# A second, turned copy of layer 0's rows, a begin without a meeting, and earlier first turns for the dilated stage

## The reference, cut to what matters

```python
def rms_norm(x, g):
    xf = x.astype(jnp.float32)
    y = xf * lax.rsqrt(jnp.mean(xf * xf, axis=-1, keepdims=True) + EPS) * g.astype(jnp.float32)
    return y.astype(x.dtype)

def conv_layer(x, conv_state, mem_kv, norm_g, w_in, conv_w, mem_q_g, w_out):
    b, t, _ = x.shape
    z = rms_norm(x, norm_g) @ w_in
    ...
```

```python
    s = jnp.einsum('brnqhe,brnkhe->brnhqk', qb, kk, preferred_element_type=jnp.float32)
    s = jnp.where(valid[None, None, :, None], s, NEG)
    m = jnp.max(s, axis=-1, keepdims=True)
    p = jnp.exp(s - m)
    l = jnp.sum(p, axis=-1, keepdims=True)
    o = jnp.einsum('brnhqk,brnkhe->brnqhe', p / l, vv.astype(jnp.float32)).astype(q.dtype)
```

## Time and profile before

| | us |
|---|---|
| median of 3 runs | 2821.64 (2819.12 to 2824.57) |
| the profiled execution | 2820.37 |
| its span in the trace | 2818.2 |
| TensorE busy | 2759.3 (98%) |
| VectorE busy | 1758.5 (62%) |
| ScalarE busy | 1113.7 (40%) |
| GpSimd busy | 364.9 (13%) |

### The profile page before, as it was taken

The page is one execution under the profiler, slowest core; times in us unless marked ns, Lnnn a source line. Parts: engine busy times, 40 slices in busy tenths (PEclk is TensorE's granted clock), DMA queues, the critical chain, the costliest instruction groups (busy, mean ns, idle before and its releaser), DMA issues.

```text
span 2818.2 us, 38685 instructions
## 1 busy us (share of the span) xinstructions
PE 2759.3 (98%) x13662; PEld 2278.4 (81%) x13662; DVE 1758.5 (62%) x3819; ACT 1113.7 (40%) x3357; POOL 364.9 (13%) x574
## 2 busy tenths in 40 slices
PE   7999999999999999999999999999999989989999
PEld 6787888888787888888787888788888779988887
DVE  5486666768678633325575767776765656557664
ACT  5433131222326224215434453532323348756532
POOL 0001010100101000000001132313324022210000
PEclk9999999999999999999999999999999999999999
DMA  4276555555676634324266676868777788647642
GB/s 169 86 239 199 190 186 175 183 181 176 199 244 205 202 106 145 99 99 150 94 250 229 224 245 226 286 219 286 262 267 246 253 283 286 215 151 244 200 142 95
DMA packets 282873, 559.16 MB, mean 198 GB/s; under 512 B 31168, under 2 KB 81920, under 8 KB 282680
## 3 DMA queue, kind: packets, MB, share of 16 engines
q1 hardware_dynamic: 248440, 453.89, 49.5%
q0 software_dynamic: 34240, 102.80, 10.0%
HBM read 423.85 MB, written 132.72 MB: 197 GB/s over the span
## 4 chain that ended last, share of the span: by engine, by line
PE 93%; DVE 3%; DMA 2%; ACT 1%; issue 1%; SPq 0%; DVEq 0%; ACTq 0%
PE ps L130 26%; PE ps L132 25%; PE ps L131 25%; PE ps L3560 2%; PE ps L3532 2%; PE ps L3081 2%; PE ps L3065 1%; PE ps L3569 1%; PE ps L3119 1%; PE ps L237 1%; PE ps L2122 1%; PE ps L2390 1%; PE ps L3548 1%; PE ps L3543 1%; DMA tok_b_dram<-shared_o 1%; PE ps L1149 1%
## 5 line engine op out<-in xcount | busy, mean ns | idle before, releaser
L130 PE MATMUL ps<-b_wp,b_sring 128*128 128x512 f32 x640 | 250.3, 391 | 4.4 <-DMA b_sring<-sums_dram 3.7
L131 PE MATMUL ps<-b_wp,b_sring 128*128 128x512 f32 x640 | 249.8, 390 | 0.0
L132 PE MATMUL ps<-b_wp,b_sring 128*128 128x512 f32 x640 | 249.7, 390 | 0.0
L130 PE MATMUL ps<-a_sring,a_wp 128*128 128x512 f32 x512 | 199.5, 390 | 2.6 <-DMA a_sring<-sums_a_dram 2.6
L132 PE MATMUL ps<-a_sring,a_wp 128*128 128x512 f32 x512 | 199.3, 389 | 0.0
L131 PE MATMUL ps<-a_sring,a_wp 128*128 128x512 f32 x512 | 199.2, 389 | 0.0
L132 PE MATMUL ps<-b_wp,b_xtlo 128*128 128x512 f32 x480 | 186.8, 389 | 0.0
L131 PE MATMUL ps<-b_wp,b_xthi 128*128 128x512 f32 x480 | 186.8, 389 | 0.0
L130 PE MATMUL ps<-b_wp,b_xthi 128*128 128x512 f32 x480 | 186.8, 389 | 0.0
L960 DVE TENSOR_TENSOR shared_o<-ps,b_spare 128x512 f32<-128x512 f32 x160 | 109.7, 685 | 100.5 <-PE ps L132 83.1
L802 ACT ACTIVATE ps<-shared_o 128x128 f32<-128x128 f32 (+1 forms) x408 | 108.0, 265 | 154.7 <-DVE shared_o L960 146.9
(11 more groups left out here) (461 smaller groups left out, 6823.5 us busy)
## 6 DMA issues: line engine op xcount, KB each, us to landing
b_sring<-sums_dram SPq DMA_DIRECT2D x160, 512.0 KB, 5.1
a_sring<-sums_a_dram SPq DMA_DIRECT2D x128, 512.0 KB, 5.0
b_raws<-w_b_dram SPq DMA_DIRECT2D x176, 256.0 KB, 4.3
a_raws<-w_a_dram SPq DMA_DIRECT2D x140, 256.0 KB, 4.4
kv_dram<-shared_o POOLq DMA_DIRECT2D x96, 256.0 KB, 4.2
tok_b_dram<-shared_o POOLq DMA_DIRECT2D x96, 256.0 KB, 4.5
front<-tok_b_dram SPq DMA_DIRECT2D x96, 256.0 KB, 3.7
front<-grp_dram SPq DMA_DIRECT2D x48, 260.0 KB, 4.3
```

The source lines that it names most:

```text
L130: pe.matmul(acc, a_hi, b_hi, start=first, stop=False)
L131: pe.matmul(acc, a_hi, b_lo, start=False, stop=False)
L132: return pe.matmul(acc, a_lo, b_hi, start=False, stop=last)
```

## The change

**Layer 0.** The rows come from the host in a second layout too: `x_turned` holds each tile of 128 rows turned, 1024 inputs as 8 x 128 partitions by 128 rows, and `xs_turned` the samples. A new class `TurnedPrep` takes the place of `Prep` in `mix_stage`. It still loads the rows as they are and squares them for the factors, but nothing of them is turned: VectorE puts the factors on a diagonal (`space`), TensorE multiplies that by a matrix of ones, which spreads the factors over all partitions (`spread_rows`, one matmul of 128 columns, 8 transposes before), VectorE scales the turned rows by them (`scale`, in two halves), ScalarE and VectorE make high and low part from it (`high`, `low`, in two halves). Rows have a ring of two tiles, turned rows one of three.

**Begin.** `Setup` registers the work of `setup_stage` in the common block; the engines wait for its semaphores and no longer meet. TensorE first makes 48 transposes of `ident`.

**Shared and dilated stage.** A new class `Opening` holds the buffers and steps that both stages use. Turning tile 0, the memory keys and tile 1 stand ahead of the fourth-last, third-last and second-last product of the shared stage, with their copies on ScalarE and VectorE; buffers are moved so that these rows are free by then. The masks are built eight products before the end. In the last phase of each pair the sample product and its output come one product earlier. SyncE loads tile 0, the memory keys, tiles 1 to 3, then values. It waits for the stored outputs ahead of the value of tile 4. ScalarE loads the table of exponentials ahead of the loop.

```diff
+class TurnedPrep:
...
+    TILES = NT + 1
+    ROWS, TURNED, RING = 2, 3, 4
+    HALF = KD // 2
...
+    def load_x(self, sp, t):
+        n, slot = self.rows(t), t % self.ROWS
+        if t >= self.ROWS:
+            sp.wait_ge(self.squared, t - self.ROWS + 1)
...
+    def loads(self, sp, gain_row, gain_src, gain_in):
+        self.load_x(sp, 0)
+        self.load_turned(sp, 0)
+        for k in range(self.RING):
+            self.load_w(sp, k)
+        self.load_x(sp, 1)
+        self.load_turned(sp, 1)
+        for k in range(self.RING, KD):
+            self.load_w(sp, k)
+        sp.dma_start(gain_row, gain_src).then_inc(gain_in, 16)
+        for t in range(2, self.TILES):
+            self.load_x(sp, t)
+            self.load_turned(sp, t)
...
+    def space(self, dve, t):
+
+        n, u = self.rows(t), t % 2
+        dve.wait_ge(self.rooted, t + 1)
+        dve.reciprocal(self.stat[0:n, u, 2:3], self.stat[0:n, u, 1:2]).then_inc(self.inverted, 1)
...
+        dve.tensor_scalar(self.diag[0:n, u, 0:n], self.core.ident[0:n, 0:n], self.stat[0:n, u, 2:3], None, ALU.mult
+                          ).then_inc(self.spaced, 1)
...
+        pe.matmul(self.factors(t), self.ones[0:n, :], self.diag[0:n, u, 0:n], start=True, stop=True).then_inc(self.spread, 1)
...
+    def begin_act(self, act):
...
+        self.square(act, 0)
+        for k in (0, 1):
+            self.split_high(act, k)
+        for half in range(2):
+            self.high(act, 0, half)
+        for k in (2, 3):
+            self.split_high(act, k)
+        self.square(act, 1)
+        for k in (4, 5):
+            self.split_high(act, k)
+        self.square(act, 2)
+        for k in (6, 7):
+            self.split_high(act, k)
+        for half in range(2):
+            self.high(act, 1, half)
...
                     if b == 0 and i + 2 <= NT:
-                        prep.low(dve, i + 2)
-                    if b == 0 and i + 4 <= NT:
-                        prep.scale(dve, i + 4)
+                        for half in range(2):
+                            prep.scale(dve, i + 2, half)
+                    if b == 0 and i + 3 <= NT:
+                        prep.space(dve, i + 3)
+                    if b == 0 and i + 2 <= NT:
+                        for half in range(2):
+                            prep.low(dve, i + 2, half)
...
-            prep.begin_pe(pe, 2)
+            pe.wait_ge(prep.setup.made, 1)
+            for _ in range(48):
+                pe.transpose(ps[:, 0, 0:P], core.ident[:, :], core.ident[:, :])
+            prep.spread_rows(pe, 0)
...
                     for k in range(KD):
+                        if b == 0 and i == 0 and k == 3:
+                            prep.spread_rows(pe, 1)
+                        if b == 0 and k == (1 if i else 7) and i + 2 <= NT:
+                            prep.spread_rows(pe, i + 2)
...
+                if n == N - 4:
+                    opening.turn(pe, 0)
+                if n == N - 3:
+                    opening.turn_memory(pe)
+                if n == N - 2:
+                    opening.turn(pe, 1)
                 product(n)
...
             for sem, count in tail.stored(tail.projected):
                 sp.wait_ge(sem, count)
-            sp.wait_ge(*tail.made)
+            sp.wait_ge(*tail.made(0))
             sp.wait_ge(*tail.split)
             sp.wait_ge(*tail.weights)
...
+            sp.wait_ge(*tail.keys)
+            opening.load(sp, 0)
+            opening.load_memory(sp)
+            for s in range(1, U):
+                opening.load(sp, s)
+            load_values(0)
+            sp.wait_ge(*tail.made(NT // 2))
+            for s in range(1, U):
+                load_values(s)
+            for s in range(U, TILES):
+                opening.load(sp, s)
+                if s == U:
                     for sem, count in tail.stored(tail.outputs[1]):
                         sp.wait_ge(sem, count)
+                load_values(s)
```

More of the change, by code:

```diff
@@ L271, in clear_samples @@
         dve.wait_ge(self.cleared, 1)
-    def begin_act(self, act, tiles):
-        self.root_table(act)
-        k = 0
-        for t in range(tiles + 2):
-            self.square(act, t)
-            if t >= 1 and t - 1 < tiles:
-                self.high(act, t - 1)
-            for _ in range(2 if k < KD else 0):
-                self.split_high(act, k)
-                k += 1
-    def begin_dve(self, dve, tiles):
-        self.clear_samples(dve)
-        k = 0
-        for t in range(tiles + 2):
-            self.scale(dve, t)
-            if t >= 1 and t - 1 < tiles:
-                self.low(dve, t - 1)
-            for _ in range(2 if k < KD else 0):
-                self.split_low(dve, k)
-                k += 1
@@ L1111, in _ @@
                 phase = j * F + f + 1
-                at_once = n < N and out_of(n) is not None and kinds[out_of(n)] == "copy"
+                at_once = n == N - 1 or n < N and out_of(n) is not None and kinds[out_of(n)] == "copy"
+                if n == N - 4:
+                    opening.copy_keys(dve, 0)
+                if n == N - 3:
+                    for m in range(MT):
+                        opening.memory_low(dve, m)
+                if n == N - 2:
+                    opening.copy_keys(dve, 1)
                 if at_once:
@@ L1687, in _ @@
                     if b == 0 and i + 2 <= NT:
-                        prep.high(act, i + 2)
-                    if b == 0 and i + 4 <= NT:
-                        prep.square(act, i + 4)
+                        for half in range(2):
+                            prep.high(act, i + 2, half)
+                    if b == 0 and i + 3 <= NT:
+                        prep.square(act, i + 3)
                     act.wait_ge(multiplied, out + 1)
@@ L3630, in build @@
         with core.holding(), nc.Block() as block:
+            setup = Setup(core, ctx, block, gains)
             with ExitStack() as st:
```

470 lines of the change are left out of this document (310 added, 160 removed).

## The result

| | kernel before | changed kernel |
|---|---|---|
| median of 18 runs each | 2820.91 us (2816.57 to 2824.57) | 2825.97 us (2821.81 to 2832.03) |
| ratio of the medians | | 1.0018, 95% interval 1.0011 to 1.0024 |
| profiled execution: time, span | 2820.37, 2818.2 us | 2827.18, 2825.4 us |

The change costs 5.1 us, 0.18%. That is within the 0.2% that I called "same", and inside my range.

What follows compares the result with a forecast made beforehand. TensorE, 93% of the chain of waits, was taken as the bound. Layer 0's +0.3 us and the dilated stage's -0.5 gave -0.2, 2821.8 beside the median, shifted to 2821.0; range 2813.5 to 2826.5.

Steps and rivals of the forecast that it cites:

- part 1: Layer 0, from the start to the second block's first matmul: terms summed to 0.3 us lost, taken as 0.3 gained.
- part 2: From the fifth-last product of the shared stage to the dilated stage's regular scores: 0.5 us lost.
- I take 5.0: Layer 0's begin: the load of x tile 2, issued at about 15.5, takes 5.0 us and lands at 20.5.
- loads are no term: Layer 0's tiles: at 211 GB/s, half of 411, and over a tile of lead, loads cost nothing.
- Rival 4: Layer 0's begin: the transposes do not raise the clock; 2823.4 us, chance 0.09.
- the ring: Layer 0's tiles: VectorE and ScalarE pass a tile back and forth, 6.2 us a tile, not 5.58; 1.6 us gained.
- Rival 3: Layer 0's tiles: a longer VectorE and ScalarE cycle; 6.7 us loses 5 us, 6.85 gives 2828; chance 0.13.
- rival 1: Layer 0's tiles: the transposes come off in full, 5.6 us a tile, 9.5 us gained, 2811.5; chance 0.10.
- the wait for the key: Behind the fifth-last shared product: TensorE waits 7.5 us for query and key tile 0; slow clock loses 2.8 more.
- the regular scores: Dilated stage: its regular scores begin 9.1 to 9.5 us after the shared stage's products end at 2302.3.
- the mark: End of the second stretch: start of the scores, 2311.07 before the change, from which the dilated stage is regular.
- Rival 2: Before the dilated stage's first turn: the key tile lands in 4 us and the clock stays up; 2815.0, chance 0.14.

Runs made afterwards that it cites:

- e6: Changed kernel with 24 transposes instead of 48 ahead of the first spread product; 2823.2 us, one run.
- e3: Changed kernel with VectorE's two low halves of a tile put ahead of the next tile's reciprocal and diagonal; 2824.71 us.
- e9: Changed kernel with ScalarE's square of the next tile put ahead of this tile's two high halves; 2818.65 us, one run.
- e8: Changed kernel with the edits of e7, and the last sample products of each pair one product earlier still; 2814.25 us, one run.
- e7: Changed kernel with SyncE's dilated-stage loads reordered: first query and key two products earlier, memory keys one, later loads moved too; 2813.97 us.
- e12: Changed kernel with dilated-stage loads reordered, sample products earlier, square before high halves, x tile 2 loaded earlier, 24 transposes; 2800.40 us.

## Why the prediction was off

**The direction.** My terms summed to 0.2 lost. The gain of 0.6 against the median came from a shift to 2821.0, because the unknowns reached further to the fast side; no term stands for it. In part 1 the terms gave 0.3 lost, and I wrote 0.3 gained for a load nearer its median; my load of 5.0 was only 0.3 above that median of 4.7, and the 0.9 has no row. The medians showed 5.1 lost, and in the traces part 2 alone lost 4.3.

**Part 1, begin.** Right in shape, off in one term. First product at 12.79 (I said 12.2); transposes cost 2.6 us and not 0.6 (diagonal ready at 7.1, spread product at 9.70), since x landed at 5.07 and not at 6.7. The term that failed is "I take 5.0" for tile 2's load. It took 7.7, and 6.4 to 7.8 in the nine other traces with this order; the load of just this place in the earlier trace rows had taken 6.4, and I stayed near the median of the earlier trace rows, which is over all 16 tiles. My sentence "loads are no term" was wrong for the begin: from 21 to 24 the DMA moved 406 GB/s, and the load stood among others. "DMA: Bandwidth & Descriptors" of the Trainium skill (Anatomy of one DMA) fits a single transfer that GpSimd issues as a fixed 2.0 us plus its bytes at 436 GB/s. An estimate by that page for 512 KB would be 3.2 us. The loads here are issued by SyncE with others behind them, and took twice that.

**Part 1, transposes.** I let them count for the clock, and the nine traces with 48 and e6 agree: the pace doubled within transposes alone. "TensorE: Matmul & The Clock Gate" of the Trainium skill (Part 4: PE-mode transpose) says that the full clock does not engage for transposes; these traces differ from it. Rival 4 is out. What I had wrong is their use: I let the clock stay up behind them until the wait for tile 2, and it fell at 14.3.

**Part 1, ring.** Right: 6.10 against 6.19, found by counting the steps from order and durations, and e3 and e9 show that it is the ring. Rival 3 is out, and rival 1 came with one line of the code moved (e9). Stretch 1 lost 0.9 in the trace and some 0.3 over six, where I had 0.3 gained: a miss of 0.6 to 1.2.

**Part 2, the wait for the key.** Right: 7.32 against 7.5, and the clock at half speed behind it, until 2291.0. The products ended 24.98 behind the fifth-last one (2279.42 to 2304.4), a little better than my 25.8.

**Part 2, behind the last product: the step that failed.** I put the regular scores at +9.1 to +9.5 behind the products; score 3 stood at 11.3, some 2.0 later, while the products ended 0.8 earlier than I had them. VectorE and ScalarE of the changed kernel there:

```profile
2303.69 0.67 DVE L1189 TENSOR_TENSOR shared_o<-shared_o,ps 8x512 f32<-8x512 f32 x1 [0.69 <-ACT shared_o L1000]
...
2305.01 1.41 DVE L1143 TENSOR_TENSOR shared_o<-ps,shared_o 128x512 f32<-128x512 f32 x2
2306.34 0.67 DVE L1147 TENSOR_TENSOR shared_o<-ps,b_spare 128x512 f32<-128x512 f32 x1
...
2309.67 0.39 ACT L3671 ACTIVATE dil_prob<-dil_prob,dil_lse 128x128 f32<-128x128 f32 x1
```

I had VectorE free for score 0. But the two additions of the sample's output (from 2303.69) and two multiplications (2305.01), of the second-last output and of the sample's, stand in front of the last output. Score 0 waits 1.49 for the first of these multiplications, the last product's output is added only at 2306.34, 1.9 behind its end, and the first minima wait for its sigmoid, so score 1 waits 1.49 more. The exponentials that I put at +3.5 began at +5.3. The sample's output that I called "gone" as a stop had only moved into VectorE's queue. e8 shows it: with the sample one product earlier score 1 stands 3.5 behind the start of the last matmul, against 5.4 in e7.

**Part 2, the mark.** Score 3 was too early a mark. What I named only as the lower bound, and put at nothing in the sum, happened: tile 5's loads stood behind the landing of the last output. SyncE issued them at 2312.46, and turn 5 waited 0.90. The wait of 1.19 I had not named at all. It is turn 9's, at the next such place in SyncE's queue, behind the loads of the memory values:

```profile
2320.05 1.28 SPq L3634 DMA_DIRECT2D b_spare<-mem_kv_dram  x2
```

In the kernel before, these were issued behind tile 3's loads, at 2294.02, when TensorE stood still anyway. With the change they went to s == V, and tile 9's key was issued only at 2324.47. The two waits cost 2.5 behind the mark. e7 moves both kinds of load and both waits are gone, so their place in the queue is the cause; which of its edits removed which wait was not tried alone. Together 0.5 lost became 4.3: 1.2 more up to score 3 and 2.5 more behind it.

**The range** held the time by 0.5 us, its upper end having been set by the ring and the clock and not by the stage that used it up. It is luck that it did. Rival 2, the fast key, is out: the key was waited for until 6.3 us after its issue. Its price of 2815.0 and the upper bound of +5.8 were also reckoned badly, since 4.1 is the length of the shorter wait and not what it saves, which is 7.5 - 4.1 = 3.4. None of my slower rivals was in part 2 at all: with the -3 of its bound and -0.3 for layer 0 the sum would have been 3.3 lost, 2825 beside the median.

## What to carry to other kernels

Work that is moved ahead of a stage's end asks for its loads earlier too: before the turn is moved, look where its load stands in the issuing engine's queue and what that queue waits for. Put the end mark of such a sum behind the last effect, not at the first regular step. And count the ring: where two engines hand a tile back and forth, the first wait on each of them shows which step can leave it at no cost.

## What the runs showed of the hardware

- The same wait of TensorE, in the same instructions, is sometimes followed by some 3 us at half pace and sometimes by none. At 874 a wait of 2.03 in the changed kernel was followed by it and one of 3.06 in e12 (at 860) by none; near 238 one of 3.64 before was followed by none and one of 3.38 in the changed kernel by slow matmuls up to 243. By itself: "TensorE: Matmul & The Clock Gate" of the Trainium skill (Part 1) says that the monitor behind the clock runs freely, so that the same kernel meets it at another phase in each run. These traces agree: in nine with the same 48 transposes the clock rose at 4.6 to 7.5.
- Transposes alone raise the clock: their pace goes from 0.213 to 0.109 us each while TensorE does nothing else, and 48 take 6.92 to 8.34.
- The raised clock is lost again in a pause: 0.50 from 9.6 on in e6, with only two small matmuls between 6.6 and 10.36.
- A load of 512 KB that SyncE issued behind four weight chunks and the gain rows, with three more of 512 KB right behind it, landed after 6.4 to 7.8 us in ten traces, at 406 GB/s in all in the changed kernel; the key tile of 256 KB, issued at 2280.44 behind the last loads of sums, was waited for until 2286.74.
